# Scores of a sample's own keys: 16 columns over a filled bank, instead of 128 columns and a mask product

## The reference

```
ckv = rmsnorm(m_kv, kv_norm_g)
krope = rope(m_kr, pos, MLA_THETA)
# samples: past is not None
ckv_all = jnp.concatenate([past[1].astype(ckv.dtype), ckv], axis=1)   # 512 cached keys + 16 own
kr_all = jnp.concatenate([past[2].astype(krope.dtype), krope], axis=1)
...
s = (einsum(q_nope, k_nope) + einsum(q_rope, k_rope)) * MLA_SCALE
p = jax.nn.softmax(s, axis=-1)        # no mask for samples: a sample sees its own 512 + 16 keys
```

## Time and profile before

| what | us |
|---|---|
| median of three runs | 1228.3 (1226.3 to 1228.69) |
| the profiled execution, its own time | 1229.02 |
| its span, first to last instruction | 1227.1 |
| PE busy in the span | 1180.7 |
| DVE busy | 617.2 |
| ACT busy | 431.1 |

### The profile page before, as it was taken

One profiled execution on the slowest core, in us unless ns is written; L12 is line 12 of the kernel. 1 busy time (PEld: TensorE's weight loads), 2 busy tenths in 40 slices (PEclk: granted clock), 3 DMA queues, 4 the chain that ended last, 5 costly groups with the idle time before them and its releaser, 6 DMA issues.

```text
span 1227.1 us, 18020 instructions
## 1 busy us (share of the span) xinstructions
PE 1180.7 (96%) x7284; PEld 1040.7 (85%) x7284; DVE 617.2 (50%) x1076; ACT 431.1 (35%) x783; POOL 65.5 (5%) x51
## 2 busy tenths in 40 slices
PE   4699999999999999999999999999999999999996
PEld 4499999999995666789999999999998566769996
DVE  3753332335538866663285233234553886666143
ACT  5452321222227434451175223122223654445010
POOL 1100001000000000002130000100000000000211
PEclk9699999999999999999999999999999999999998
DMA  9912111112023543365121211111212242116012
GB/s 345 375 35 73 34 34 50 35 36 57 19 92 95 172 147 112 118 232 175 46 91 58 73 34 34 50 35 36 65 28 95 100 147 77 44 34 240 1 69 86
DMA packets 72062, 112.96 MB, mean 92 GB/s; under 512 B 3617, under 2 KB 55977, under 8 KB 70706
## 3 DMA queue, kind: packets, MB, share of 16 engines
q1 hardware_dynamic: 71986, 111.92, 26.9%
HBM read 94.43 MB, written 16.42 MB: 90 GB/s over the span
## 4 chain that ended last, share of the span: by engine, by line
PE 89%; DVE 6%; ACT 1%; DMA 1%; SPq 1%; issue 1%; DVEq 0%; POOLq 0%; POOL 0%; ACTq 0%
PE psum L911 55%; PE psum L1246 6%; PE psum L1299 5%; PE psum L1278 3%; PE psum L1199 3%; PE psum L1189 1%; PE psum L902 1%; DMA modw<-in_w_mod 1%; PE psum L1313 1%; PE psum L1236 1%; DVE w_lo L1843 1%; DVE h_lo L1793 1%; PE psum L1295 1%; PE psum L1235 1%; PE psum L1085 1%; PE psum L1253 1%
## 5 line engine op out<-in xcount | busy, mean ns | idle before, releaser
L911 PE MATMUL psum<-h_hi,w_hi 128*128 128x384 f32 x1392 | 473.8, 340 | 5.2 <-DVE ckvT L1845 2.5
L911 PE MATMUL psum<-h_hi,w_lo 128*128 128x384 f32 x1392 | 466.3, 335 | 0.0
L911 PE MATMUL psum<-h_lo,w_hi 128*128 128x384 f32 x1392 | 466.3, 335 | 0.0
L911 PEld LDWEIGHTS psum<-h_hi,w_hi 128*128 128x128 f32 x1392 | 262.2, 188 | 11.0 <-issue 7.8
L911 PEld LDWEIGHTS psum<-h_hi,w_lo 128*128 128x128 f32 x1392 | 262.4, 188 | 0.5 <-issue 0.5
L911 PEld LDWEIGHTS psum<-h_lo,w_hi 128*128 128x128 f32 x1392 | 262.2, 188 | 0.0
L1843 DVE TENSOR_TENSOR w_lo<-raw,w_hi 128x1024 fp32r<-128x1024 f32 x61 | 77.3, 1268 | 204.9 <-ACT w_hi L1450 204.1
L1450 ACT ACTIVATE w_hi<-raw 128x1024 fp32r<-128x1024 f32 (+1 forms) x62 | 65.3, 1053 | 258.2 <-PE psum L911 178.9
L1299 PE MATMUL psum<-pT,ckv 128*128 128x512 f32 x144 | 74.0, 598 | 1.6 <-DVE pT L1846 1.2
L1514 ACT ACTIVATE probs_p<-psum,nmax 128x128 f32<-128x128 f32 (+1 forms) x72 | 25.1, 361 | 121.3 <-DVE esink L1843 121.3
L748 POOL TENSOR_TENSOR sq_a<-sq_a,sq_a 128x768 f32<-128x768 f32 x12 | 22.1, 1842 | 764.1 <-ACT sq_a L1393 764.1
(11 more groups left out here) (226 smaller groups left out, 1443.2 us busy)
## 6 DMA issues: line engine op xcount, KB each, us to landing
raw<-in_w_in SPq DMA_DIRECT2D x18, 1024.0 KB, 5.4
raw<-in_w_mod SPq DMA_DIRECT2D x15, 1024.0 KB, 5.2
x<-xT_scratch SPq DMA_DIRECT2D x4, 2304.0 KB, 10.5
modw<-in_w_mod SPq DMA_DIRECT2D x8, 1024.0 KB, 15.0
raw<-in_w_out SPq DMA_DIRECT2D x10, 768.0 KB, 5.1
tab<-in_c_rope SPq DMA_DIRECT2D x6, 1152.0 KB, 6.8
tok<-in_x_prompt SPq DMA_DIRECT2D x2, 2048.0 KB, 10.1
ckvT_c<-in_cache_mla_ckvT SPq DMA_DIRECT2D x8, 512.0 KB, 3.6
```

The lines of the kernel that those rows point to most:

```text
L911: mm = pe.matmul(psum[:, bank, 0:BLK], w_[:, k, :], h[:, k, blk(n)], start=(k == 0 and i == 0), stop=(k == KD - 1 and i == 2))
```

## The change

The samples' second bank is no longer computed in full. DVE fills its 128 columns with -1e30 (a new instruction, 128x128, L2033 of the changed kernel), and PE then computes only the 16 own columns of each sample, over the filled ones. The mask products go, with their constants, their DMA, and the rounding on DVE. The fill stands in DVE's list behind the `norm` step of job `BANKS_FREE[j]`, and `scores(j)` waits for it by the new semaphore `sample_own_scores_emptied` before its first product, that with the cached keys included. It is made four times a layer.

```diff
                     else:
                         pe.wait_ge(mlc_in[t].sem, mlc_in[t].at(lane.layer, 16 * 3))
                         pe.wait_ge(qas_ok.sem, qas_ok.at(lane.layer, 2))
-                        for a, e in ((0, 512), (512, 640)):
+                        pe.wait_ge(own_neg.sem, own_neg.at(lane.layer, t + 1))
+                        for own in range(2):
                             for s, half in enumerate(HALVES):
-                                keys = ckvT_c[t % 2][:, s, :] if a == 0 else ckvT[:, SEQ:NTOK]
-                                pe.matmul(out[half, a:e], qas[:, 2 * t + s, :], keys, start=True, stop=False)
+                                b = TS * (2 * t + s)
+                                a, w = (512 + b, TS) if own else (0, 512)
+                                keys = ckvT[:, SEQ + b:SEQ + b + TS] if own else ckvT_c[t % 2][:, s, :]
+                                pe.matmul(out[half, a:a + w], qas[:, 2 * t + s, :], keys, start=True, stop=False)
...
-                        for s, half in enumerate(HALVES):
-                            mm = pe.matmul(out[half, 512:640], own8[:, TS * (2 * t + s):TS * (2 * t + s) + 1].broadcast_to([NB, 64]),
-                                           block_mask, start=False, stop=True)
...
                     ts(p_view(j), p_view(j), rinv[:, s, 0:1], None, ALU.mult, sig=p_ok)
+                    for i in range(PAIRS_S):
+                        if BANKS_FREE[GROUPS[INDEX["s", i]]["jobs"][0]] == j:
+                            lane.link(dve.memset(psum[:, banks_of(GROUPS[INDEX["s", i]]["jobs"][0])[1], 0:P], NEG), own_neg)
...
-            sp.dma_start(masks_f[:], io["c_masks"]).then_inc(s_const.sem, 16)
...
-            dve.wait_ge(s_const.sem, 32)
-            dve.tensor_copy(masks[:], masks_f[:]).then_inc(s_cst.sem, 1)
-            dve.wait_ge(s_cst.sem, 6)
+            dve.wait_ge(s_const.sem, 16)
+            dve.wait_ge(s_cst.sem, 5)
```

More of the change, by code:

```diff
@@ L324, in build @@
     state = sm("state", [P, 2, 2 + 2 * NB])
-    masks = sm("masks", [8, 2 * P], BF16)
     edge = sm("edge", [P, 2 * CH], BF16)
@@ L348, in build @@
     qr_lo = at("qr_lo", SPL_AT + 15360, [P, 2, P], F32R)
-    masks_f = at("masks_f", ZT_AT, [8, masks.shape[1]])
-    own8, block_mask = masks[:, 0:P], masks[:, P:2 * P]
     psum = nc.alloc_psum_tensor("psum", [P, 8, 512], F32)
@@ L426, in build @@
     pt_c = [sg("probs_turned_copied_by_scalar", COPIER.count(0)), sg("probs_turned_copied_by_vector", COPIER.count(1))]
+    own_neg = sg("sample_own_scores_emptied", PAIRS_S)
     pv = sg("values_weighted", NUNITS)
@@ L741, in _ @@
             pool.memset(cT[:], 0.0).then_inc(s_cst.sem, 1)
-            pool.wait_ge(s_cst.sem, 6)
+            pool.wait_ge(s_cst.sem, 5)
             def add_squares(lane, sq, base):
@@ L847, in turn_y_end @@
                             mm.then_inc(s_yT.sem, 1)
-            pe.wait_ge(s_const.sem, 32)
-            pe.wait_ge(s_cst.sem, 6)
+            pe.wait_ge(s_const.sem, 16)
+            pe.wait_ge(s_cst.sem, 5)
             bank = 0
@@ L1249, in scores @@
                         pe.wait_ge(qas_ok.sem, qas_ok.at(lane.layer, 2))
-                        for a, e in ((0, 512), (512, 640)):
+                        pe.wait_ge(own_neg.sem, own_neg.at(lane.layer, t + 1))
+                        for own in range(2):
                             for s, half in enumerate(HALVES):
-                                keys = ckvT_c[t % 2][:, s, :] if a == 0 else ckvT[:, SEQ:NTOK]
-                                pe.matmul(out[half, a:e], qas[:, 2 * t + s, :], keys, start=True, stop=False)
+                                b = TS * (2 * t + s)
+                                a, w = (512 + b, TS) if own else (0, 512)
+                                keys = ckvT[:, SEQ + b:SEQ + b + TS] if own else ckvT_c[t % 2][:, s, :]
+                                pe.matmul(out[half, a:a + w], qas[:, 2 * t + s, :], keys, start=True, stop=False)
                             for s, half in enumerate(HALVES):
-                                keys = krT_c[t % 2][half, :] if a == 0 else krT[half, SEQ:NTOK]
-                                mm = pe.matmul(out[half, a:e], qrs[half, t, :], keys, start=False, stop=(a == 0))
-                        for s, half in enumerate(HALVES):
-                            mm = pe.matmul(out[half, 512:640], own8[:, TS * (2 * t + s):TS * (2 * t + s) + 1].broadcast_to([NB, 64]),
-                                           block_mask, start=False, stop=True)
+                                b = TS * (2 * t + s)
+                                a, w = (512 + b, TS) if own else (0, 512)
+                                keys = krT[half, SEQ + b:SEQ + b + TS] if own else krT_c[t % 2][half, :]
+                                mm = pe.matmul(out[half, a:a + w], qrs[half, t, :], keys, start=False, stop=True)
                     mm.then_inc(score.sem, 1)
@@ L2201, in constants @@
 def constants():
[L2203 to L2207, removed]
     pos = np.concatenate([np.arange(1024), np.tile(512 + np.arange(16), 8)]).astype(np.float32)
@@ L2215, in constants @@
         rope[i, :, 1] = np.concatenate([-sin, sin, -sin, sin])
-    return {"c_ident": np.eye(128, dtype=np.float32), "c_masks": masks,
-            "c_rope": rope}
+    return {"c_ident": np.eye(128, dtype=np.float32), "c_rope": rope}
 def kernel(**inputs):
```

## The result

The changed kernel takes 1239.57 us (median of 4 runs, 1238.44 to 1245.69), the kernel before 1228.43 us (median of 4 runs beside it, 1226.30 to 1228.69). The ratio is 1.0105 with a 95% interval of 1.0069 to 1.0141: slower by 11.1 us. Predicted were 1242.8 us, and 1236 to 1247. The profiled execution took 1240.69 us, with a span of 1238.8 us.

What follows compares the result with a forecast made beforehand. PE was taken as the bound, with DVE nearly full. From 1229.0 us: -3.4 jobs, -0.4 start, +13.1 waits, +5.2 clock gave 1243.5; the profiled execution lay 0.7 above the median, so 1242.8, range 1236 to 1247.

Steps and rivals of the forecast that it cites:

- PE bounds the stage, and a wait on it isn't given back: Sample attention: PE is full, so each us taken from it or waited on it changes the run by one us.
- Rival (b): Sample attention: PE's lead over DVE is worth nothing, so only 3.8 us of removed work count: 1224.5 us, chance 0.04.
- The waits: PE ahead of the sample pairs' scores: 4.76 and 4.77 us at first pairs, 1.61 and 1.96 at third, 13.1 in all.
- The fill: DVE's 128x128 fill of PSUM: 0.18 us, 0.26 with hand-overs; DVE's eight fills in its idle time except where PE waits.
- The upper bound of the waits: PE's waits at the sample pairs if each fill takes 0.82 us: 16.5 us.
- (c): Rival, longer: the fill takes 0.8 us in PSUM, 1247.0 us, or the half clock lasts longer, 1249.6 us; chance 0.08.
- The narrow products: Own-key products on PE at 16 columns: 0.24 us a group, saving 0.43 us a job with the mask, -3.4 us in eight.
- The start: Kernel start: without the mask DMA's issue, later issues move up; -0.4 us, bounds 0 and -0.8.
- The clock: PE's clock falls to half behind each layer's first sample pair wait, 5.5 us each: 5.2 us for two.
- (a): Rival at the first sample pairs: the waits come but the clock holds, 1237.6 us; chance 0.14.
- the prediction's own factor of 0.47: Share of PE work time under the half clock that is lost: 1 - 1.93 / 3.64, from 32 products at both clocks.
- The sum: Whole profiled execution: 1229.0 - 3.4 - 0.4 + 13.1 + 5.2 = 1243.5 us; median expected 1242.8.

Runs made afterwards that it cites:

- the wait alone: The kernel before with only the DVE fill and PE's wait for it added at the changed kernel's places, full-width products and masks kept: 1244.42 us, ratio 1.0130.
- removed work alone: The changed kernel without the fill and the wait for it, so the other 112 columns go unmasked: 1225.07 us, ratio 0.9968.
- the early fills alone: The kernel before with only four fills placed earlier in DVE's list and PE's wait for them, full-width products and masks kept: 1229.76 us, ratio 1.0012.

## Why the prediction was right, point by point

- **PE bounds the stage, and a wait on it isn't given back.** Right for the waits: the table of starts shows each one kept to the end, and taking them out by an earlier fill gave back 13.2 us. Rival (b), the wait that is only moved, is excluded by that and by the wait alone (+15.4). Too strong was the other half of the sentence, that each us taken from PE shortens the run by one. From the first to the second pair PE's lead on DVE is under half a us: removed work alone leaves that distance at 21.98 us. DVE's 5.38 of 6.00 us is not slack of a tenth: the rest are the gaps from one DVE instruction to the next (0.62 us over 16 instructions, 0.04 each), and a further instruction doesn't fit into them: the early fill of 0.17 us cost 0.26.
- **The waits.** Predicted 4.76, 4.77, 1.61, 1.96 and twice none per layer, 13.1 us; measured 4.85, 4.85, 1.71, 2.05, 13.4 us in all. Comparing PE's start with the end of the DVE step ahead of the fill was enough. The hand-overs were 0.10 and 0.14 us rather than 0.03 and 0.05.
- **The fill.** Taken at 0.18 us, measured 0.165 us. That DVE's fills lie in its idle time was wrong for the stretch between the first and the second pair, as the early fills alone show (1.2 us); in the changed kernel PE's wait hides it. The upper bound of the waits was added up wrongly too: with a fill of 0.82 us the four come to 13.1 + 4 x 0.64 = 15.7 us, with 0.4 us at the fourth pair of layer two 16.1 and not 16.5, and (c) then counts 0.8 a second time. It should read 1245.8 and not 1247.0. The top of the range stood on it; the forecast doesn't, and what was measured lies well below either.
- **The narrow products.** Taken at 0.24 us a group, measured 0.22; so a job saves 0.47 us and not 0.43: 3.8 us in eight for 3.4. The Trainium skill, "TensorE: Matmul & The Clock Gate", section "Wait — 56ns, not 53.3ns?", puts the floor from start to start at about 25 ns; here four products of 16 columns take 0.22 us, 55 ns each, near the 0.20 us of their four weight loads. The row was the better guide.
- **The start.** Taken at -0.4 us. PE's first product came at 9.53 to 9.81 us in the seven traces without the mask DMA, and at 9.86 to 10.04 in the three with it: some 0.3 us. Whether they reach the end no run shows, since PE comes to the first pair at 413.18 to 416.00 us in the three traces with that DMA and at 415.29 to 416.88 in six of those without. The 0.7 us of this execution agree with the term but don't confirm it.
- **The clock: the term that was mis-sized.** In the profile it fell at both first pairs, as forecast (both falls, not (a)), but cost 1.6 + 2.0 = 3.6 us and not 5.2. The factor was right and the length wrong: I took 5.5 us of work under half clock for each fall, there were 3.4 and 4.4. By the prediction's own factor of 0.47 these give 1.6 and 2.05 us. The clock was also read too narrowly in the trace before. The prediction counts two falls and has no row for a short wait, but there is a third, from 58.1 to 64.9 us, right behind a stretch of 3.40 us in which PE was busy 1.99 us and waited 1.47 us at one piece (ahead of 56.11). So a fall behind the third pairs' waits of 1.7 and 2.05 us deserved a chance of its own; it came in two of the other kernels.
- **The sum.** The profiled execution (1240.69) lies 2.8 us under the sum (1243.5): -1.6 of the clock, -0.4 of the jobs, -0.3 of the start, +0.3 of the waits, -2.0 in all. The 0.8 us that remain lie in two places (0.9 by the rounded figures). From the end of the first pair's job to the second pair it takes 18.83 and 18.81 us, before 19.05 and 19.07: 0.5 us for the two layers together. Another 0.4 lie between the fourth pair of layer one and the first of layer two (5.83 - 0.47 + 4.85 = 10.21, and the table has 9.80); 0.16 of these are a wait for DVE ahead of 621.15 us in the trace before that is not there now. The cause of the rest stays open. The median lies 3.2 us under its own forecast of 1242.8; that this has the same reasons is argued from one execution and not shown.

What stays open: what decides whether a wait of 1.7 to 2.7 us is followed by the half clock. The same wait was, and was not, in one execution (2.74 us in two layers), and for the times without a profile only the mean clock is known. I can't say how many falls the median of 1239.57 us holds. The four runs of the changed kernel spread over 7 us: the slowest, 1245.69 us, had a mean clock of 0.977, the others 0.984 and 0.985.

## What to carry to other kernels

An operation that is moved from a full engine to another costs the hand-over first: ask at what time the new engine can have done it in its order, against the time at which the old one starts, and price that wait before the saving. Here 3.8 us in eight jobs were bought with 13.4 us of wait, though the fill takes 0.17 us and needed nothing from the `norm` that it stood behind. Give such a step to the engine that makes the condition true (here ScalarE, whose `exp` frees the bank) and that has room; and where two engines are nearly balanced, a gain on one counts only as far as its lead over the other.

## What was not expected of the hardware

- The half clock (0.50) came after waits of 1.70 us in two profiles and after 2.74 us in one, but not after 1.71 and 2.05 us in others, and not after 2.74 us in the other layer of the same profile. At the sample pairs it came after 3.41 us and more each of six times.
- It can begin while PE is still waiting (1004.20, PE starts at 1006.64), and then costs less. The cost is that of the work under it: 3.4 us cost 1.6, 4.4 cost 2.0, 6.0 cost 2.8.
- PE comes to the first sample pair, less its wait there, at 413.18 to 416.88 us in the traces of nine kernels that give it the same work up to there. A difference of one or two us between two profiles is read from a place, not from their ends.
- ScalarE's copy of a constant into PSUM (128x128) takes 0.28 us against 0.165 us of DVE's fill, and was the cheaper in the kernel.
